# Casting the next weight tile before the attention units of a step, instead of behind them

## What is computed

```python
h = rmsnorm(x, norm1)
proj = h @ w_in            # q (12 heads) | k (4) | v (4) | ... | merge gates A and B
qa = apply_rope(rmsnorm(qa)) * HEAD_DIM_A ** -0.5
ka = apply_rope(rmsnorm(ka))
# three groups, (window, dilation) = (128,1), (512,4), (2048,16)
for g in groups:
    s = q_g @ k.T (masked);  m = max(s);  p = exp(s - m);  den = sum(p)
    o_g = p @ v / den;  lse_g = m + log(den)
oa = sum over g of softmax(lse)_g * o_g
y = sigmoid(ga) * (oa @ w_proj_a) + sigmoid(gb) * (ob @ w_proj_b)
```

## Time and profile before

| what | value |
|---|---|
| median of 3 runs | 1840.6 us (1839.83 to 1841.87) |
| the profiled execution: own time | 1840.6 us |
| its span, first to last instruction | 1839.0 us |
| TensorE matmul busy | 1783.5 us, 97% |
| VectorE / ScalarE / GpSimd busy | 1084.8 / 701.8 / 487.1 us |
| mean granted TensorE clock | 0.996 of full |
| attention phase | about 79 to 551 us, four heads of 118 us |

### The profile page before, as it was taken

One profiled execution on the slowest core, in us unless ns is written; L12 is line 12 of the kernel. 1 busy time (PEld: TensorE's weight loads), 2 busy tenths in 40 slices (PEclk: granted clock), 3 DMA queues, 4 the chain that ended last, 5 costly groups with the idle time before them and its releaser, 6 DMA issues. The chain is left out here.

```text
span 1839.0 us, 27056 instructions
## 1 busy us (share of the span) xinstructions
PE 1783.5 (97%) x9188; PEld 1514.9 (82%) x9188; DVE 1084.8 (59%) x1928; ACT 701.8 (38%) x1598; POOL 487.1 (26%) x578
## 2 busy tenths in 40 slices
PE   6999999999999999999989999989999999999999
PEld 5888888888888888888867888868888888878887
DVE  4353553644637758484956455685555555566776
ACT  5333343243334353443544223453333333344443
POOL 3010101101017242332411000016655566420220
PEclk9999999999999999999999999999999999999999
DMA  7312412413122102111136233313233232288774
GB/s 207 89 39 64 106 63 66 124 63 110 63 69 88 47 24 65 27 57 29 48 100 235 80 86 98 137 64 105 89 108 114 97 108 86 86 287 310 238 229 166
DMA packets 169294, 196.35 MB, mean 107 GB/s; under 512 B 9552, under 2 KB 119472, under 8 KB 168704
## 3 DMA queue, kind: packets, MB, share of 16 engines
q1 hardware_dynamic: 156816, 163.13, 27.7%
q0 software_dynamic: 6128, 21.74, 3.6%
q10 hardware_dynamic: 6272, 10.49, 1.5%
HBM read 150.88 MB, written 44.45 MB: 106 GB/s over the span
## 5 line engine op out<-in xcount | busy, mean ns | idle before, releaser
L2240 PE MATMUL bank<-act_hi,w_hi 128*128 128x512 f32 x568 | 228.6, 403 | 4.0 <-DVE act_lo L1874 3.8
L2242 PE MATMUL bank<-act_hi,w_lo 128*128 128x512 f32 x568 | 222.3, 391 | 0.0
L2241 PE MATMUL bank<-act_lo,w_hi 128*128 128x512 f32 x568 | 221.7, 390 | 0.0
L2240 PE MATMUL bank<-ca,wq 128*128 128x512 f32 x528 | 206.7, 391 | 6.4 <-DVE wq L1985 4.0
L2241 PE MATMUL bank<-ca,wq 128*128 128x512 f32 x528 | 206.2, 390 | 0.0
L2242 PE MATMUL bank<-ca,wq 128*128 128x512 f32 x528 | 206.1, 390 | 0.0
L2240 PE MATMUL bank<-w_hi,act_hi 128*128 128x256 f32 (+1 forms) x576 | 179.9, 312 | 2.9 <-DVE act_lo L1557 2.9
L2242 PE MATMUL bank<-w_hi,act_lo 128*128 128x256 f32 (+1 forms) x576 | 176.7, 307 | 0.0
L2241 PE MATMUL bank<-w_lo,act_hi 128*128 128x256 f32 (+1 forms) x576 | 176.6, 307 | 0.0
L2240 PEld LDWEIGHTS bank<-act_hi,w_hi 128*128 128x128 f32 x568 | 107.1, 189 | 27.5 <-DVE act_lo L1874 4.8
L2242 PEld LDWEIGHTS bank<-act_hi,w_lo 128*128 128x128 f32 x568 | 106.9, 188 | 23.1
(11 more groups left out here) (357 smaller groups left out, 4221.3 us busy)
## 6 DMA issues: line engine op xcount, KB each, us to landing
w_raw<-in_w_in SPq DMA_DIRECT2D x60, 512.0 KB, 4.0
rawd<-in_w_ffn_down SPq DMA_DIRECT2D x99, 256.0 KB, 5.0
rx<-y_scratch SPq DMA_DIRECT2D x77, 256.0 KB, 4.3
wr<-in_w_ffn_gate SPq DMA_DIRECT2D x11, 1024.0 KB, 5.4
wr<-in_w_ffn_up SPq DMA_DIRECT2D x11, 1024.0 KB, 5.3
y_scratch<-sq SPq DMA_DIRECT2D x11, 1024.0 KB, 4.3
y_scratch<-yq SPq DMA_DIRECT2D x33, 256.0 KB, 2.0
gate_scratch<-gbuf ACTq DMA_DIRECT2D x32, 256.0 KB, 2.0
```

The costliest lines, as they stand in the source:

```text
L2240: pe.matmul(ps, lhs_hi, rhs_hi, start=first, stop=False, skip_group_check=onto)
L2241: pe.matmul(ps, lhs_hi, rhs_lo, start=False, stop=False, skip_group_check=onto)
L2242: return pe.matmul(ps, lhs_lo, rhs_hi, start=False, stop=last, skip_group_check=onto)
```

## The change

In the steps from 8 on, two blocks of instructions change places, on ScalarE and on VectorE. ScalarE now makes the cast `hi_a` directly behind the gate copy and its store, ahead of the copy of `qk_t` (steps 8 and 9), the `pt` copies and the exponentials of the step. VectorE now makes `lo_a`, and in heads 1 to 3 `merge_mul`, ahead of the step's `dve_unit` calls. TensorE's, GpSimd's and SP's instructions are the same, and so are all waits.

```diff
@@ act_head_a
-                if s < 8:
-                    for k in HI_A.get(s, []):
-                        hi_a(k % 4, 2 * h + k // 4 + 2)
+                for k in HI_A.get(s, []):
+                    hi_a(k % 4, 2 * h + k // 4 + 2)
                 if 2 <= s < 10:
...
-                if s >= 8:
-                    for k in HI_A.get(s, []):
-                        hi_a(k % 4, 2 * h + k // 4 + 2)
                 if behind and s == 1:
                     act_weights(h - 1)
@@ dve_head_a
                 if s < 8:
                     qk_norm(s)
                     rope(s)
-                for j in UNITS_AT.get(s, []):
-                    dve_unit(j)
-                if s >= 8:
+                else:
                     for k in HI_A.get(s, []):
                         lo_a(A0 + TA * h + k, k % 4)
                     if behind and s in MUL_AT:
                         merge_mul(h - 1, MUL_AT[s])
+                for j in UNITS_AT.get(s, []):
+                    dve_unit(j)
```

## The result

The changed kernel takes 1864.9 us (median of 4 runs, 1861.71 to 1868.87), the kernel before 1841.2 us beside it (4 runs, 1839.83 to 1842.52). The ratio is 1.013, with a 95% interval of 1.0105 to 1.0154: 1.3% slower. The profiled execution, a fifth one, is the shortest: 1860.7 us with a span of 1859.0 us.

A forecast was written before the change was run, and what follows sets the result against it. TensorE, busy 97% of the span, was taken as the bound. Waits of 0.4 + 0.45 + 1.6 + 2.1 = 4.55 us a head, 18.2 in four, on 1840.6 gave 1858.8, rounded to 1858.5; range 1851 to 1866.

The forecast's parts named there:

- likeliest case: Attention phase: TensorE's new waits in steps 10, 11, 13 and 14 and nothing else, giving 1858.5 us.
- the clock rival's case: TensorE's clock falls in the new pauses: one fall a head adds 6 us, 1864.8; some or all heads, 23 in 100.
- Nothing to win from an earlier `w_lo`: Attention phase: no TensorE wait is for `w_lo`, so making cast and subtraction earlier gains nothing.
- Step 13, 1.6 us: Units 10 and 11, tile 8: `u_t` copy ends later, so the weight load of `pe_pv(8)` waits; 1.6 us a head.
- Step 14, 2.1 us: Units 12 and 13, tile 9: `pe_pv(10)` loads 2.1 us late a head, including 0.95 from the later `pt` copy.
- Steps 10 and 11, 0.4 and 0.45 us: Tiles 6 and 7: later `u_t` copies delay `pe_pv(2)` by 0.4 us (bounds 0.2 to 0.55) and `pe_pv(4)` by 0.45.
- Step 8 and `merge_mul`, nothing: Unit 2, tile 5: delays covered by step 9's stream; `merge_mul` in steps 9 and 12 beside a stream; no cost.
- The sum, 18.2 us: Steps 10, 11, 13 and 14 add 4.55 us a head, 18.2 us in four heads.
- The time outside the phase, unchanged: A sign of being right: time outside the attention phase stays the same; a changed time after 551 us means wrong.
- Main case: The four steps' waits and nothing else, 1855 to 1861.5 us; 58 in 100.
- the worst case: A second clock fall in each head, in step 13, adds another 6 us: 1871.

The follow-up runs named there:

- ScalarE's part alone: Against the kernel before: only ScalarE's cast moved as in the changed kernel, VectorE's order as before; 1845.1 us, ratio 1.0018.
- `merge_mul` alone: Against the kernel before: only `merge_mul` moved ahead of the units of steps 8, 9 and 12, casts and subtractions as before; 1842.0 us, ratio 1.0007.
- steps 8 to 12 together: Against the kernel before: both engines' orders changed in steps 8 to 12 only, steps 13 and 14 as before; 1843.0 us, ratio 1.0009.
- step 14 alone: Against the kernel before: both engines' orders changed in step 14 only, steps 8 to 13 as before; 1851.4 us, ratio 1.0057.
- subtraction one unit later: Against the changed kernel: VectorE's subtraction put behind the first unit of each step, ScalarE as in the changed kernel; 1845.4 us, ratio 1.0025.

## Why the prediction was right, and where its likeliest case was not

The sign, the mechanism and the place were as forecast, and 1864.9 lies in the range of 1851 to 1866. The likeliest case, 1858.5, was 6.4 us low, and its own span of 1855 to 1861.5 missed: what was measured is the clock rival's case, 1864.8, which had 23 in 100.

Its steps, by what the trace and the experiments gave:

- Nothing to win from an earlier `w_lo`: right. No wait of TensorE in the phase before was for one, and none shows up as removed.
- Step 13, 1.6 us: the weight load that stood 2.80 us behind the gate copy stands at 307.21 now, 4.36 behind it: 1.56.
- Step 14, 2.1 us with 0.95 of it from the `pt` copy: the weight load that stood 1.63 us behind the gate copy stands at 317.16, 3.73 behind it: 2.1. The `pt` copy's part is 0.9, shown by the experiment with ScalarE's part alone.
- Steps 10 and 11, 0.4 and 0.45 us: 0.2 and 0.4. The longer way from mask to copy of step 10 (1.14 us in the earlier trace rows) did not come back: it took 0.75. I had taken the middle of two bounds; it was the lower one.
- Step 8 and `merge_mul`, nothing: right as far as the runs can tell. `merge_mul` alone makes no difference that can be told, and steps 8 to 12 together cost 2.0 us, no more than the pauses of steps 10 and 11.
- The sum, 18.2 us: about 16.8 in the traces. The kernel that keeps TensorE at work through the pauses, 17.9 over the kernel before, measures the waits without the clock in this phase.
- The time outside the phase, unchanged: 1.2 us less in the profiled execution, beside one fall of the clock fewer.

The step that failed is the weight given to the clock: "Main case 58 in 100; clock falls in some or all heads 23". The falls are the rule here. In the profiled executions of the changed kernel there were falls in two and in three of the four heads, and filling the pauses takes 5.8 us off the median. The price that I gave to one fall in every head, 6 us, fits the 5.8 us, but not in that shape: some heads have none, others one, two or three falls. So it is partly luck that 1864.8 and 1864.9 agree: the waits came out 1.4 us smaller than summed, and the number of falls changes from execution to execution.

What misled me is that I took the pair of the earlier trace rows, one pause of 1.32 us with no fall and one of 2.46 with a fall, as two lengths between which the clock decides, and left step 13, whose pause is as short as the first, to the worst case. The traces don't bear this out on either side. The pause of 1.32 us in step 13 was followed by a fall in three of the eight heads of the two profiled executions, as often as the pauses of step 14. And the long pause of the earlier trace rows, in the changed kernel:

```profile
630.56 1.80 PE L2431 MATMUL lvl_ps<-fbuf 128*128 128x128 f32 x14 [2.45 <-DVE lvm L1797]
```

The same 2.45 us, and the group behind it takes 1.80 us at full clock. It was so in both profiled executions of the changed kernel; in those of the other eight kernels a fall followed. The one profile that I had before the prediction couldn't show that a pause of one length goes both ways.

By the Trainium skill ("TensorE: Matmul & The Clock Gate", "What's actually happening") idleness halves the clock and sustained work brings it back; the windows at 0.50 behind the pauses agree, and so does the kernel in which the pauses are filled.

What stays open is why the same pause is followed by a fall in one head, or one execution, and not in the next. Step 13's part of the loss wasn't run alone; it is what is left of the others, and read from the trace.

## What to carry to other kernels

Engines that are busy for a third and a half of the time (ScalarE and VectorE in the earlier trace rows) can still hold up the one that is busy all the time: before moving work forward on them, look at what stands behind the new place in their order and how much slack that has, not at how much idle time there is. Work that must first wait for something (here a subtraction that waits for a cast of the same step) is best put behind the first result that the busy engine wants; one unit later, it cost nothing that could be told. Price a new pause of TensorE by its length plus the chance of a lowered clock behind it (here 16.8 us of pauses and 5.8 of clock), and don't take one trace with a fall, or without, for a rule about the pause's length.

## What the runs showed of the hardware that I had not expected

The same pause sometimes brings the clock to 1.2 GHz and sometimes not. In the profiled executions:

| pause of TensorE | a fall behind it |
|---|---|
| 1.3 us, step 13 (changed kernel, two executions) | 3 of 8 |
| 1.73 and 0.97 us, 0.44 us of transposes between, step 14 (changed kernel, and step 14 alone) | 6 of 12 |
| 1.73 us alone, step 14 (ScalarE's part alone; subtraction one unit later) | 0 of 8 |
| 2.45 to 2.51 us, (ten executions of nine kernels) | 8 of 10 |
| 1.3 us, (the same ten) | 0 of 10 |

So the length of a pause alone doesn't decide it, and with the second pause in step 14 falls were more frequent than with the first alone. Transposes that compute nothing, 33 a head, cost no time of their own and made the kernel 5.8 us quicker and its times steadier.
